# One-hot rows of four tokens by one instruction in the spreading of gates

## The chip, the cores and the metric

One core of one Trainium2 chip runs the whole program. The metric is the device time of one execution in microseconds; the kernel before took 4191.1 us in the median of three runs (4186.91 to 4193.54).

## The reference

Two layers of a decoder trunk over 512 tokens of width 1024. Each layer has a token mixer (four branches, gates, projections) and then PEER, a feed-forward network of 16384 experts, addressed by a row key and a column key out of 128 each. Only PEER bears on this change:

```
top_s, pos = lax.top_k(cand, PEER_TOPK)
eidx = jnp.take_along_axis(cidx, pos, axis=-1)      # row * 128 + column
gate = jax.nn.softmax(top_s, axis=-1)
hidden = jax.nn.gelu(jnp.einsum('td,thkd->thk', xb, u_tab[eb]))
return jnp.einsum('thk,thkd->td', gb * hidden, v_tab[eb])
```

For each token 8 heads pick 16 experts each, so there are 128 pairs (expert, gate) a token. The kernel computes all 16384 experts densely for 384 of the 512 tokens, and multiplies by a matrix of gates that is zero where an expert wasn't picked. The first 128 tokens are done by gathering their picked rows instead.

## The kernel before, in words

A layer goes through stages, each a block of its own for all engines: mixers, merge, query, routing (`route_stage`), spreading of gates (`spread_stage`), experts (`experts_stage`). The change is in `spread_stage`, which runs once in each layer.

The routing leaves three tiles of 128 x 384: `rowT`, `colT` and `gateT`. Partition p of column t holds the row key, the column key and the gate of pair p of token t. The spreading makes of each token a 128x128 matrix (row key by column key) of gates, by one matmul: the stationary operand is one-hot over the row keys of the token's 128 pairs (`hot_row`), the moving one is one-hot over the column keys, times the gate (`hot_col`), and the sum over the 128 pairs is the matrix.

The work goes in turns of STEP = 16 tokens, 24 turns a layer, and each turn in four groups of four tokens (`g` = 0 to 3). Group g has its own PSUM bank and its own four slots of `hot_row` and `hot_col`, used again in the next turn. In a turn:

- VectorE (lines 1400 to 1418) copies 16 columns of `colT`, `rowT` and `gateT` into `cols`, writes the four `hot_row` tiles of group 0 by four 128x128 compares (L1410), and all sixteen `hot_col` tiles by a compare and a multiplication in one instruction each (L1412). In every second turn it also makes a low part of expert weights by a 128x1024 subtraction, behind group 1 (L1044).
- ScalarE writes `hot_row` of group 1 another way (L1451 to L1457, distance and ReLU), evicts each bank (L1464), and makes high parts and the GELU for the experts that are computed ahead.
- GpSimd (L1389 to L1392) writes `hot_row` of groups 2 and 3: a copy of four columns of `rowT` into `rows`, a drain, and four 128x128 compares against `iota_row`, each with one column of `rows` as its scalar.
- TensorE (L1435) does the four matmuls of a group once `hot_row` and `hot_col` are there and the bank has been evicted, and half an expert chunk's multiplication behind group 1 (L86 to L88).
- SyncE stores the finished gates in DRAM and loads expert weights ahead.

All order is by semaphores written out by hand. `spread` counts groups multiplied and frees their slots; `rows_hot` counts GpSimd's groups, `rows_hot_a` ScalarE's, `cols_hot` VectorE's; `kept` counts evictions. VectorE starts group g of a turn when TensorE has multiplied group g of the turn before, and GpSimd likewise.

Of the kernel before, what the change touches and what calls it, by code (L numbers as in the profile page):

```python
# [1340 lines left out]
def spread_stage(nc, a, layer, sb, sem, bank, x, ur, load_next, iota_row, rowT, colT, gateT):  # L1341
# [5 lines left out]
    with ExitStack() as ctx:  # L1347

        ahead = HiddenAhead(nc, a, layer, ctx, sb, sem, bank, x, ur, load_next, "sp", AHEAD_ROUTE)
        hot_row = sb(ctx, "hot_row", [P, STEP, P])  # L1350
        hot_col = sb(ctx, "hot_col", [P, STEP, P])
        cols = sb(ctx, "cols", [P, 3, STEP])
        rows = sb(ctx, "rows", [P, 2, 4])
        row_of = sb(ctx, "row_of", [P, 4])
        distance = sb(ctx, "distance", [P, 4, P])
        stage = sb(ctx, "stage", [P, 2, P, TB])
        rows_hot = sem("sp_rows_hot")
        rows_hot_a = sem("sp_rows_hot_a")
        cols_hot = sem("sp_cols_hot")
        chain_a = sem("sp_chain_a")  # L1360
        spread = sem("sp_spread")
        kept = sem("sp_kept")
        stored = [sem(f"sp_stored{b}") for b in range(2)]
        chain = sem("sp_chain")
        TURNS = TB // STEP

        def unrolled(eng, body):

            def pair(m, last):
                for b in range(2):  # L1370
                    for q in range(TURNS):
                        body((2 * m + b) * TURNS + q, b, q, m, last)
            with eng.Fori(0, NTB // 2 - 1) as m:
                pair(m, False)
            pair(NTB // 2 - 1, True)

        def two_ahead(step, eng, b, q, m, last, turn):

            if q % 2 == turn and not (b == 1 and last):
                step(eng, m + b, (2 * b + q // 2 + 2) % EC)  # L1380

        with nc.Block() as block:

            @block.gpsimd
            def _(pool):
                def body(n):
                    for g in range(2, 4):
                        pool.wait_ge(spread, 4 * n + g + 1)
                        nc.gpsimd.tensor_copy(rows[:, g % 2, :], rowT[:, ds(n * STEP + 4 * g, 4)])  # L1389
                        pool.drain()  # L1390
                        for s in range(4):
                            ins = nc.gpsimd.tensor_scalar(hot_row[:, 4 * g + s, :], iota_row[:], rows[:, g % 2, s:s + 1], None, ALU.is_equal)  # L1392
                        ins.then_inc(rows_hot, 1)

                with pool.Fori(0, NTB * TURNS) as n:
                    body(n)

            @block.vector
            def _(dve):
                def body(n, b, q, m, last):  # L1400
                    dve.wait_ge(cols_hot, 4 * n + 4)
                    nc.vector.tensor_copy(cols[:, 0, :], colT[:, ds(n * STEP, STEP)])
                    nc.vector.tensor_copy(cols[:, 2, :], rowT[:, ds(n * STEP, STEP)])
                    nc.vector.tensor_copy(cols[:, 1, :], gateT[:, ds(n * STEP, STEP)]).then_inc(chain, 1)
                    dve.wait_ge(chain, n + 1)
                    for g in range(4):
                        dve.wait_ge(spread, 4 * n + g + 1)
                        if g == 0:
                            for s in range(4 * g, 4 * g + 4):
                                nc.vector.tensor_scalar(hot_row[:, s, :], iota_row[:], cols[:, 2, s:s + 1], None, ALU.is_equal)  # L1410
                        for s in range(4 * g, 4 * g + 4):
                            ins = nc.vector.tensor_scalar(hot_col[:, s, :], iota_row[:], cols[:, 0, s:s + 1], cols[:, 1, s:s + 1],  # L1412
                                                          ALU.is_equal, ALU.mult)
                        ins.then_inc(cols_hot, 1)
                        if g == 1:
                            two_ahead(ahead.low, dve, b, q, m, last, 1)

                dve.sem_inc(cols_hot, 4)
                dve.sem_inc(ahead.u_low, 4)
                for c in range(2):  # L1420
                    ahead.low(dve, 0, c)
                unrolled(dve, body)

            @block.tensor
            def _(pe):
                def body(n, b, q, m, last):
                    for g in range(4):
                        pe.wait_ge(kept, 4 * n + g + 1)
                        if g == 1:
                            pe.wait_ge(rows_hot_a, n + 1)  # L1430
                        if g >= 2:
                            pe.wait_ge(rows_hot, 2 * n + g - 1)
                        pe.wait_ge(cols_hot, 4 * n + g + 5)
                        for s in range(4):
                            mm = nc.tensor.matmul(bank[g][:, s * P:(s + 1) * P], hot_row[:, 4 * g + s, :], hot_col[:, 4 * g + s, :],  # L1435
                                                  start=True, stop=True)
                        mm.then_inc(spread, 1)
                        if g == 1:
                            part = slice(q % 2 * KT // 2, (q % 2 + 1) * KT // 2)
                            ahead.multiply(pe, m, 2 * b + q // 2, part)  # L1440

                pe.sem_inc(spread, 4)
                pe.sem_inc(ahead.h_mm, 4)
                unrolled(pe, body)

            @block.scalar
            def _(act):
                def one_hot_rows(n):

                    act.wait_ge(spread, 4 * n + 2)  # L1450
                    nc.scalar.activation(row_of[:], rowT[:, ds(n * STEP + 4, 4)], ACT.Copy).then_inc(chain_a, 1)  # L1451
                    act.wait_ge(chain_a, 2 * n + 1)
                    for s in range(4):
                        ins = nc.scalar.activation(distance[:, s, :], iota_row[:], ACT.Abs, scale=-1.0, bias=row_of[:, s:s + 1])
                    ins.then_inc(chain_a, 1)
                    act.wait_ge(chain_a, 2 * n + 2)
                    nc.scalar.activation(hot_row[:, 4:8, :], distance[:], ACT.Relu, scale=-1.0, bias=1.0).then_inc(rows_hot_a, 1)  # L1457

                def body(n, b, q, m, last):
                    two_ahead(ahead.high, act, b, q, m, last, 0)  # L1460
                    act.wait_ge(stored[b], 16 * m + 16)
                    for g in range(4):
                        act.wait_ge(spread, 4 * n + g + 5)
                        nc.scalar.activation(stage[:, b, :, q * STEP + 4 * g:q * STEP + 4 * g + 4],  # L1464
                                             bank[g][:].rearrange("p (t c) -> p c t", t=4), ACT.Copy).then_inc(kept, 1)
                        if g == 1 and not (last and b == 1 and q == TURNS - 1):
                            one_hot_rows(n + 1)
                        if g == 2 and q % 2 == 1:
                            ahead.gelu(act, m, 2 * b + q // 2)

                act.sem_inc(kept, 4)
                act.sem_inc(stored[0], 16)
                act.sem_inc(stored[1], 16)
                act.sem_inc(ahead.h_act, 4)
                for c in range(2):
                    ahead.high(act, 0, c)
                one_hot_rows(0)
                unrolled(act, body)

            @block.sync  # L1480
            def _(sp):
                def pair(m, last):
                    if not last:
                        for r in range(2):
                            ahead.load(sp, m + 1, r)
                    else:
                        ahead.load_for_next_stage(sp, AHEAD_SPREAD)
                    for b in range(2):
                        ahead.store(sp, m, b)
                        sp.wait_ge(kept, (2 * m + b) * 4 * TURNS + 4 * TURNS + 4)  # L1490
                        sp.dma_start(a["gates"][:, :, 2 * m + b], stage[:, b].rearrange("p (g c) t -> p g c t", c=EC)).then_inc(stored[b], 16)

                for r in range(2):
                    sp.sem_inc(ahead.h_out[r], 16)
                with sp.Fori(0, NTB // 2 - 1) as m:
                    pair(m, False)
                pair(NTB // 2 - 1, True)
# [864 lines left out]
```

## Time and profile before

| what | value |
|---|---|
| median of three runs | 4191.1 us |
| the profiled execution, its own time | 4191.99 us |
| its span, first to last instruction | 4190.3 us |
| mean granted TensorE clock, share of full | 0.960 |
| ScalarE busy | 1483.8 us (35%) |
| GpSimd busy | 1312.4 us (31%) |
| GpSimd `hot_row` compares L1392, 128x128, 384 of them | 254.2 us, mean 676 ns |
| VectorE `hot_row` compares L1410, 128x128, 192 of them | 44.6 us, mean 302 ns |
| TensorE `hot_col` x `hot_row` L1435, records | 1536, 191.1 us |

A row of the profile names the line, the engine, the operation, output and input tiles with their shapes, and the number of instructions. In a list in order of time the first column is the start and the second the duration in microseconds; a row with x4 stands for four instructions in a row, and the duration runs from the start of the first to the end of the last. A bracket at the end is idle time of the engine before the row, and what ended it. Instructions of one engine overlap a little: the next can start before the one ahead has ended, so the step between two starts is the time that one costs in a full queue. DVE is VectorE, POOL is GpSimd, ACT is ScalarE, PE is TensorE.

### The profile page before, as it was taken

Reading aid. Unit: us, or ns where it says so; the run is one execution under the profiler, and the core shown is the slowest. Engines: PE = TensorE matmul, PEld = TensorE weight load, DVE = VectorE, ACT = ScalarE, POOL = GpSimd, SP = SyncE. Lnnn points to the kernel's source line nnn. Section 1 sums busy time; section 2 is a strip of 40 time slices with the busy share of each in tenths; the row PEclk is TensorE's granted clock in tenths of the full one; section 3 lists DMA queues with packets and bytes.
Section 4 is the critical chain, followed back from the end, with each engine's and each line's share of the span. In section 5 each row is a group of like instructions: output and inputs, shape, how many; then the busy total and the mean of one; then the engine's idle time right before and its main releaser. Section 6 shows DMA issues by size and latency. Waiting matters only on the chain. (4 is left out here: it accounts for less than half of the span.)

```text
span 4190.3 us, 55217 instructions
## 1 busy us (share of the span) xinstructions
PE 3896.6 (93%) x19618; PEld 3407.1 (81%) x19618; DVE 2799.5 (67%) x5400; ACT 1483.8 (35%) x2136; POOL 1312.4 (31%) x1140
## 2 busy tenths in 40 slices
PE   8987899999789999999899878999997899999996
PEld 7865687899788999988778566878997889999885
DVE  3254434479997888877642644343899888888776
ACT  2232322234573333333321323222445633333332
POOL 1010000056574555532100100000666755555321
PEclk9997899999899999999999978999999999999998
DMA  3210323244369999999622103222444699999994
GB/s 141 80 57 1 111 93 113 106 149 174 124 217 360 354 354 338 345 338 333 234 102 80 58 1 118 96 103 106 160 168 147 231 358 355 358 340 344 334 331 173
DMA packets 263243, 836.41 MB, mean 200 GB/s; under 512 B 19617, under 2 KB 68769, under 8 KB 237985
## 3 DMA queue, kind: packets, MB, share of 16 engines
q1 hardware_dynamic: 189344, 565.82, 37.8%
q0 software_dynamic: 73728, 268.47, 17.4%
q8 instruction: 89, 1.46, 0.1%
q14 instruction: 82, 0.66, 0.0%
HBM read 749.81 MB, written 84.41 MB: 199 GB/s over the span
## 5 line engine op out<-in xcount | busy, mean ns | idle before, releaser
L1044 POOL TENSOR_TENSOR ahead_u_low<-merged,ahead_u_high 128x1024 fp32r<-128x1024 f32 x96 | 255.5, 2678 | 1241.4 <-ACT ahead_u_high L1039 1241.4
L87 PE MATMUL bank<-v_high,w_high 128*128 128x512 f32 x1536 | 598.1, 389 | 0.0
L86 PE MATMUL bank<-v_low,w_high 128*128 128x512 f32 x1536 | 598.1, 389 | 0.0
L88 PE MATMUL bank<-v_high,w_low 128*128 128x512 f32 x1536 | 597.4, 389 | 0.0
L1089 POOL DMA_INDIRECT far_rows<-peer_v_dram,far_index x256 | 370.4, 1447 | 503.5 <-DVE x_far L1113 458.9
L1089 POOL DMA_INDIRECT far_rows<-peer_u_rows_dram,far_index x256 | 368.0, 1437 | 346.0 <-DVE far_dots L1095 295.4
L1731 DVE TENSOR_TENSOR v_low<-v_raw,v_high 128x1024 fp32r<-128x1024 f32 x256 | 301.9, 1221 | 231.4 <-ACT v_high L1670 231.4
L1670 ACT ACTIVATE v_high<-v_raw 128x1024 fp32r<-128x1024 f32 x256 | 257.1, 1052 | 499.0 <-PE bank L88 493.4
L86 PE MATMUL bank<-xT_low,u_high 128*128 128x384 f32 x1088 | 372.1, 342 | 19.2 <-ACT hid L1658 10.0
L88 PE MATMUL bank<-xT_high,u_low 128*128 128x384 f32 x1088 | 371.2, 341 | 0.0
L87 PE MATMUL bank<-xT_high,u_high 128*128 128x384 f32 x1088 | 371.1, 341 | 0.0
L1113 DVE SCALAR_TENSOR_TENSOR x_far<-far_rows,far_dots,x_far 128x1024 f32<-128x1024 f32 x256 | 328.1, 1282 | 23.6 <-DMA far_rows<-peer_v_dram,far_index 10.0
L88 PEld LDWEIGHTS bank<-v_high,w_low 128*128 128x128 f32 x1536 | 288.4, 188 | 60.4
L86 PEld LDWEIGHTS bank<-v_low,w_high 128*128 128x128 f32 x1536 | 288.4, 188 | 59.2
L87 PEld LDWEIGHTS bank<-v_high,w_high 128*128 128x128 f32 x1536 | 288.4, 188 | 58.5
L86 PE MATMUL bank<-xT_low,ahead_u_high 128*128 128x384 f32 x960 | 329.5, 343 | 0.0
L87 PE MATMUL bank<-xT_high,ahead_u_high 128*128 128x384 f32 x960 | 324.0, 337 | 0.0
L88 PE MATMUL bank<-xT_high,ahead_u_low 128*128 128x384 f32 x960 | 323.9, 337 | 0.0
L1095 DVE CUSTOM_DVE_ANT_0 far_rows<-far_rows,x_far 128x1024 f32<-128x1024 f32 x256 | 302.5, 1220 | 18.6 <-DMA far_rows<-peer_u_rows_dram,far_index 18.1
L1664 ACT ACTIVATE w_high<-hid 128x384 fp32r<-128x384 f32 x256 | 128.9, 526 | 443.2 <-DVE hid L1722 443.2
L1392 POOL TENSOR_SCALAR hot_row<-iota_row,rows 128x128 f32<-128x128 f32 x384 | 254.2, 676 | 16.3 <-issue 16.3
L1435 PE MATMUL bank<-hot_col,hot_row 128*128 128x128 f32 x1536 | 191.1, 281 | 40.3 <-DVE hot_col L1412 22.9
(356 smaller groups left out, 8520.4 us busy)
## 6 DMA issues: line engine op xcount, KB each, us to landing
merged<-peer_u_dram SPq DMA_DIRECT2D x128, 1024.0 KB, 7.2
v_raw<-peer_v_dram SPq DMA_DIRECT2D x128, 1024.0 KB, 7.9
gates_scratch<-stage SPq DMA_DIRECT2D x12, 4096.0 KB, 14.4
G<-gates_scratch SPq DMA_DIRECT2D x64, 768.0 KB, 7.8
in_raw<-w_in_dram SPq DMA_DIRECT2D x40, 1024.0 KB, 6.2
mg_raw<-w_merge_dram SPq DMA_DIRECT2D x52, 768.0 KB, 4.2
hidden_scratch<-ahead_hid SPq DMA_DIRECT2D x60, 384.0 KB, 2.4
hid<-hidden_scratch SPq DMA_DIRECT2D x30, 768.0 KB, 7.1
```

Source lines behind the costliest of these rows:

```text
L86: nc.tensor.matmul(out, lh, rl, start=first, stop=False)
L87: nc.tensor.matmul(out, lh, rh, start=False, stop=False)
L88: return nc.tensor.matmul(out, ll, rh, start=False, stop=last)
L1044: eng.tensor_tensor(self.ul[:, c], self.ur[:, c], as_f32(self.uh[:, c]), ALU.subtract).then_inc(self.u_low, 1)
L1089: pool.indirect_dma_start(self.rows[:, m % RING, :], None, self.tables[m // PAIRS], bass.IndirectOffsetOnAxis(ap=self.index[:, slot:slot + ...
L1095: self.nc.vector.tensor_tensor_reduce(out=row, in0=row, in1=self.x[:], scale=1.0, scalar=0.0, op0=ALU.mult, op1=ALU.add, accum_out=self.do ...
L1113: self.nc.vector.scalar_tensor_tensor(out=self.x[:], in0=self.rows[:, m % RING, :], scalar=self.dots[:, m - PAIRS:m - PAIRS + 1], in1=self ...
L1392: ins = nc.gpsimd.tensor_scalar(hot_row[:, 4 * g + s, :], iota_row[:], rows[:, g % 2, s:s + 1], None, ALU.is_equal)
L1435: mm = nc.tensor.matmul(bank[g][:, s * P:(s + 1) * P], hot_row[:, 4 * g + s, :], hot_col[:, 4 * g + s, :], start=True, stop=True)
L1664: A(wh[:, b, c, :], hid[:, b, c, :], ACT.Copy).then_inc(w_high, 1)
L1670: A(vh[:, c:c + 2, cols(r)], vr[:, c:c + 2, cols(r)], ACT.Copy).then_inc(v_high, 1)
L1731: V.tensor_tensor(vl[:, c:c + 2, cols(r)], vr[:, c:c + 2, cols(r)], as_f32(vh[:, c:c + 2, cols(r)]), ALU.subtract).then_inc(v_low, 1)
```

## The change

GpSimd's copy into `rows` and its four 128x128 compares a group become two instructions of 128x512. The first subtracts the four tokens' row keys, each repeated over 128 columns, from `iota_row`, repeated four times, with both operands read from SBUF by patterns with a step of zero. The second, behind the drain, compares the result in place with 0.0. VectorE's four 128x128 compares of group 0 become one 128x512 compare of the same two patterns, and its copy of `rowT` into `cols` goes. The tile `rows` goes, and `cols` is a third smaller. Nothing changes in the waits and the counts, nor in the column compares.

```
             def _(pool):
                 def body(n):
                     for g in range(2, 4):
+                        four = hot_row[:, 4 * g:4 * g + 4, :]
                         pool.wait_ge(spread, 4 * n + g + 1)
-                        nc.gpsimd.tensor_copy(rows[:, g % 2, :], rowT[:, ds(n * STEP + 4 * g, 4)])
+                        nc.gpsimd.tensor_tensor(four, iota_row[:].unsqueeze(1).to_broadcast([P, 4, P]),
+                                                rowT[:, ds(n * STEP + 4 * g, 4)].unsqueeze(2).to_broadcast([P, 4, P]),
+                                                ALU.subtract)
                         pool.drain()
-                        for s in range(4):
-                            ins = nc.gpsimd.tensor_scalar(hot_row[:, 4 * g + s, :], iota_row[:], rows[:, g % 2, s:s + 1], None, ALU.is_equal)
-                        ins.then_inc(rows_hot, 1)
+                        nc.gpsimd.tensor_scalar(four, four, 0.0, None, ALU.is_equal).then_inc(rows_hot, 1)
...
                     nc.vector.tensor_copy(cols[:, 0, :], colT[:, ds(n * STEP, STEP)])
-                    nc.vector.tensor_copy(cols[:, 2, :], rowT[:, ds(n * STEP, STEP)])
                     nc.vector.tensor_copy(cols[:, 1, :], gateT[:, ds(n * STEP, STEP)]).then_inc(chain, 1)
...
                         if g == 0:
-                            for s in range(4 * g, 4 * g + 4):
-                                nc.vector.tensor_scalar(hot_row[:, s, :], iota_row[:], cols[:, 2, s:s + 1], None, ALU.is_equal)
+                            nc.vector.tensor_tensor(hot_row[:, 0:4, :], iota_row[:].unsqueeze(1).to_broadcast([P, 4, P]),
+                                                    rowT[:, ds(n * STEP, 4)].unsqueeze(2).to_broadcast([P, 4, P]), ALU.is_equal)
```

## Rows read from the trace of the kernel before

**Rows 1.** The page's first part: busy time of each engine.
```profile
PE 3896.6 (93%) x19618; PEld 3407.1 (81%) x19618; DVE 2799.5 (67%) x5400; ACT 1483.8 (35%) x2136; POOL 1312.4 (31%) x1140
```

**Rows 2.** Busy time by stretch: the stage in each layer.
```profile
core 0: us, PE busy (x) PEld busy (x) DVE busy (x) ACT busy (x) POOL busy (x), PEclk, DMA share, GB/s
1088.10:1249.50 161.40, 144.51 (x1056) 142.01 (x1056) 148.88 (x563) 116.36 (x258) 133.02 (x237) 0.96 0.53 182
3174.10:3332.40 158.30, 142.82 (x1056) 140.51 (x1056) 148.73 (x563) 116.18 (x258) 133.82 (x237) 0.97 0.54 186
```

**Rows 3.** VectorE in order of time, two turns: start, us, engine, line, operation.
```profile
1195.94 0.17 DVE L1402 COPY cols<-colT 128x16 f32<-128x16 f32 x1
1196.03 0.17 DVE L1403 COPY cols<-rowT 128x16 f32<-128x16 f32 x1
...
1196.31 0.91 DVE L1410 TENSOR_SCALAR hot_row<-iota_row,cols 128x128 f32<-128x128 f32 x4
1197.13 4.49 DVE L1412 TENSOR_SCALAR hot_col<-iota_row,cols 128x128 f32<-128x128 f32 x16
1201.66 0.31 DVE L1402 COPY cols<-colT 128x16 f32<-128x16 f32 x1
...
1202.26 0.98 DVE L1410 TENSOR_SCALAR hot_row<-iota_row,cols 128x128 f32<-128x128 f32 x4
1203.16 2.21 DVE L1412 TENSOR_SCALAR hot_col<-iota_row,cols 128x128 f32<-128x128 f32 x8
1205.30 1.21 DVE L1044 TENSOR_TENSOR ahead_u_low<-merged,ahead_u_high 128x1024 fp32r<-128x1024 f32 x1
...
1208.85 0.17 DVE L1402 COPY cols<-colT 128x16 f32<-128x16 f32 x1
```

**Rows 4.** GpSimd in order of time, same stage, first layer.
```profile
1154.14 0.24 POOL L1389 COPY rows<-rowT 128x4 f32 x1 [5.66 <-PE bank L1435]
...
1201.58 2.39 POOL L1392 TENSOR_SCALAR hot_row<-iota_row,rows 128x128 f32<-128x128 f32 x4 [0.17 <-issue]
1204.78 0.26 POOL L1389 COPY rows<-rowT 128x4 f32 x1 [0.81 <-PE bank L1435]
1205.21 3.50 POOL L1392 TENSOR_SCALAR hot_row<-iota_row,rows 128x128 f32<-128x128 f32 x4 [0.17 <-issue]
```

**Rows 5.** VectorE in order of time: mixers and routing.
```profile
256.25 2.31 DVE L2169 COPY tmp<-tmp 128x6 f32<-128x6 f32 x1
...
881.70 0.68 DVE L1287 TENSOR_TENSOR hits<-best 128x512 f32<-128x512 f32 x1
882.30 0.55 DVE L1290 TENSOR_TENSOR hits<-best 128x384 f32<-128x384 f32 x1
...
892.10 1.61 DVE L1308 TENSOR_TENSOR pgate<-top 128x128 f32<-128x128 f32 x1
...
894.75 0.29 DVE L1315 TENSOR_TENSOR rankf<-rankf 128x128 f32<-128x128 f32 x1
```

**Rows 6.** GpSimd in order of time, beside rows 5.
```profile
256.14 4.73 POOL L1873 TENSOR_TENSOR gl_wl<-gl_raw,gl_wh 128x1024 fp32r<-128x1024 f32 x2 [4.93 <-ACT gl_wh L1869]
...
891.16 2.40 POOL L1044 TENSOR_TENSOR ahead_u_low<-merged,ahead_u_high 128x1024 fp32r<-128x1024 f32 x1 [1.75 <-ACT ahead_u_high L1039]
```

**Rows 7.** GpSimd's groups by line and shape: count, busy us, mean ns.
```profile
L1922 POOL TENSOR_SCALAR_AFFINE_SELECT ws<-ws 128x512 f32<-128x512 f32 x2 | 1.3, 630 | 0.0
L169 POOL TENSOR_SCALAR_AFFINE_SELECT lvl_mask<-lvl_mask 128x128 f32<-128x128 f32 x4 | 1.2, 308 | 0.3
```

**Rows 8.** VectorE in order of time, while GpSimd waits.
```profile
1150.01 0.88 DVE L1410 TENSOR_SCALAR hot_row<-iota_row,cols 128x128 f32<-128x128 f32 x4
1150.80 2.14 DVE L1412 TENSOR_SCALAR hot_col<-iota_row,cols 128x128 f32<-128x128 f32 x8
1152.86 1.22 DVE L1044 TENSOR_TENSOR ahead_u_low<-merged,ahead_u_high 128x1024 fp32r<-128x1024 f32 x1
```

**Rows 9.** VectorE's groups by line and shape: the column compare.
```profile
L1412 DVE TENSOR_SCALAR hot_col<-iota_row,cols 128x128 f32<-128x128 f32 x768 | 215.6, 352 | 0.1
```

More of the change, by code:

```diff
@@ L1351, in spread_stage @@
         hot_col = sb(ctx, "hot_col", [P, STEP, P])
-        cols = sb(ctx, "cols", [P, 3, STEP])
-        rows = sb(ctx, "rows", [P, 2, 4])
+        cols = sb(ctx, "cols", [P, 2, STEP])
         row_of = sb(ctx, "row_of", [P, 4])
```

## The prediction

> **What bounds the kernel now.** The page's first part [rows 1] shows TensorE busy 93% of the span and VectorE 67%, an average over stages with different limits. The change touches one stage only, so I went on to the table of busy time by stretches for the two times it runs (once for each layer) [rows 2]: 161.4 and 158.3 us, 319.7 us of 4190.3. In it VectorE is busy 148.9 of 161.4 us and GpSimd 133.0. A layer has 24 turns of 16 tokens, so a turn takes 6.7 us on average.
>
> Next comes VectorE in order of time, for two turns late in the first layer [rows 3]. The reader is to see that it never stops: a turn that begins at 1195.94 ends at 1201.66 (5.72 us), the next one, with a 128x1024 subtraction in it, ends at 1208.85 (7.19 us). No row has an idle time. 12.91 us for two turns, 6.45 for one: VectorE sets the pace. GpSimd in the same stretch [rows 4] is nearly as full: four compares of 128x128 take 2.39 us, each group pays 0.17 us for the drain, and it waits 0.81 us for TensorE once in two turns. So anything that is added to VectorE in this stage lengthens it at once, and about 0.4 us a turn is what GpSimd could lose before it binds too.
>
> **What the change removes from VectorE.** One copy of 128x16, 0.09 us from its start to the next one's (1195.94 to 1196.03). Four one-hot compares of 128x128: 0.82 us (1196.31 to 1197.13) and 0.90 us (1202.26 to 1203.16), mean 0.86 [rows 3]. It adds one compare of 128x512 with two tensor inputs. A 128x512 operation on two SBUF inputs with broadcast patterns is in the trace: it starts at 881.70, and the next one at 882.30 [rows 5], so 0.60 us. VectorE's own work falls by 0.09 + 0.86 - 0.60 = 0.35 us a turn.
>
> **What it does on GpSimd.** Out: a copy of 128x4, and four compares of 128x128, for each of two groups a turn. In: a subtraction of 128x512 with two tensor inputs, the drain (stays at 0.17 us), and one compare of 128x512 against a constant. No row shows either at that size. The subtraction: 128x1024 takes 2.40 us in [rows 6]. Half of it, 1.2 us, is the low bound, the whole 2.4 the high one; the nearest row is twice its size, so I take 1.3. The compare: GpSimd's one-input operation of 128x512 (affine select) takes 630 ns and that of 128x128 308 ns [rows 7], 0.84 ns a column; a 128x128 compare takes 600 ns undisturbed (2.39 us for four, [rows 4]), so 0.60 + 384 x 0.00084 = 0.92 us; low bound 0.63 us (the affine select), high bound 2.4 us (four times the small one). A group takes 1.3 + 0.17 + 0.92 = 2.4 us, against 0.43 (copy and drain, 1204.78 to 1205.21, [rows 4]) + 2.39 = 2.8 before. By its own work GpSimd gains 0.4 us a group.
>
> **What the two do to each other.** This is the term that decides. At 256.14 GpSimd begins two subtractions of 128x1024, 4.73 us together [rows 6]. At 256.25 VectorE begins a copy of six columns, and it takes 2.31 us [rows 5]. At 891.16 GpSimd begins another one, which ends at 893.56; a VectorE operation of 128x128 that began at 892.10 ends at 893.71, after 1.61 us, where a like one takes 0.29 (894.75). So VectorE stands still until GpSimd's whole instruction is through, and then has 0.15 us to go: of its own 0.29 us, 0.14 were spent while it waited. The other way round, GpSimd's four compares take 3.50 us instead of 2.39 when VectorE's subtraction of 1.21 us falls into them (1205.21 in [rows 4], 1205.30 in [rows 3]).
>
> Now, why does the stage not suffer from this today, with GpSimd comparing all the time? Because the compares are short. With GpSimd idle (it waits 5.66 us until 1154.14, [rows 4]) VectorE's four row compares take 0.79 us and eight column compares 2.06 (1150.80 to 1152.86, [rows 8]), 0.257 us each; with GpSimd at work sixteen take 4.49 (1197.13 to about 1201.62, [rows 3]) instead of 4.11. That is 0.38 us on sixteen plus about 0.07 on the four; 0.45 us spread over eight GpSimd compares is 0.056 us for each. Nearly all of the 600 ns of a small compare leaves VectorE free.
>
> After the change GpSimd has four long instructions in a turn instead of eight short ones. For the subtraction I take the part that shuts VectorE out as half of 2.31 us, 1.16 us, less the 0.14 us that VectorE spends usefully: 1.02 us. Bounds: 0 (if these patterns don't shut it out) and 2.2. For the compare: what a small one costs, 0.056, plus 384 columns at 0.84 ns, 0.38 us. Bounds: 0 and its whole duration of 0.92. Two groups a turn: 2 x (1.02 + 0.38) = 2.80 us. The 0.38 us of today's disturbance on the column compares goes. Net for a turn: 2.80 - 0.38 - 0.35 = +2.07 us, a turn of 8.5 us. The first turn of a layer has its GpSimd groups ahead of VectorE's work and the last turn's fall largely behind it, so 23 turns in each of the two layers pay: 46 x 2.07 = +95 us.
>
> Is GpSimd or TensorE then the bound in place of VectorE? GpSimd: 4.8 us for two groups, 0.6 for the mean share of VectorE's 1.2 us subtraction, about 0.5 for its new compare: 5.9 of 8.5. TensorE is busy 144.5 us in 24 turns [rows 2], 6.0 us a turn, and has room. What waits behind VectorE's stalled compare is its column compares, the group's matmuls after them, and ScalarE's eviction; all of them are late by the same amount and none adds. The stage's block ends before the next stage works, and that one's load of the gates waits for the last store, so I find nothing that gives the time back.
>
> The Trainium skill, "SBUF — State Buffer", section "Who interferes with whom", speaks against this change: GpSimd shares a port pair with VectorE, and whichever starts first holds it for the whole of its instruction, against VectorE's two-input operations and its two-port modes (which it lists tensor_scalar under). The rows agree for a copy and for two-input operations; for VectorE's tensor_scalar against a long GpSimd instruction the trace of before has no row. By the rule taken literally, with each GpSimd instruction's whole duration, the small compares of today would have to stop VectorE for 0.6 us each, and what was worked out above from the rows is 0.056.
>
> The same skill, "GPSIMD Engine Reference", section 3.1, gives 4497 ns for a two-input operation of 2048 columns. An estimate from that page with this trace's 2.40 us for 1024 is 1.37 us for 512 columns; put in for 1.3 it would move the sum by under 8 us.
>
> **The time.** The profiled execution took 4191.99 us (span 4190.3) and the median is 4191.1, so they can be read as one. 4192 + 95 = 4287 us, in the median's terms 4286.
>
> **Rivals.**
> A. The port is shared only against operations with two tensor inputs and copies, and VectorE's tensor_scalar compares pass beside GpSimd (no row shows one stopped for long; the 0.056 us may be other things). Then VectorE saves 0.35 us a turn, GpSimd 0.8, and TensorE with 6.0 is close behind: 48 x 0.35 = 17 us less, 4175. Against it: the column compares do get slower when GpSimd is at work. It decides if column compares keep their mean [rows 9]. Chance 0.10.
> B. Only the subtraction shuts VectorE out, the compare against a constant doesn't, or the waits fall into gaps: 2 x 1.02 - 0.73 = 1.31 us a turn, +60, 4252. For it: a small compare leaves VectorE free for most of its duration. Chance 0.20.
> C. GpSimd's instructions hold it for their whole duration: 2 x (1.3 - 0.14 + 0.92) - 0.73 = 3.43 us a turn, +158, 4350. For it: the copy at 256.25 was stopped 0.11 us after GpSimd's start. Chance 0.15.
> D. The compare of 128x512 costs four small ones, 2.4 us, and holds as long: GpSimd 2 x 3.9 us a turn, VectorE's 5.7 plus 2 x (1.02 + 2.3) = 12.3 a turn, +5.9, +270, 4460. Chance 0.05.
> The forecast has 0.50. TensorE's clock could add to C and D: granted 0.96 and 0.97 of full on average in this stage [rows 2]; a turn with more idle time may see the lower of its two levels (1.2 GHz) more often. I give that no price of its own.
>
> The range reaches from 4235, below B, to 4355, just past C; outside are A and D and a little of B: 0.2. A measurement of this kernel can tell 0.2%, 8.4 us, from no change. Slower: forecast, B, C, D, 0.90, less a little for mishaps between A and B: 0.88. Faster: most of A, 0.09. Same: 0.03.
>
> **What would show it.** In the changed profile: the mean of VectorE's 128x128 column compare, 352 ns before [rows 9], rises to about 500 ns (2.8 us over sixteen and the rest), with single ones over 1 us; GpSimd's subtraction near 1.3 us and its compare near 0.9; the stage some 48 us longer in each layer; TensorE's waits in it for VectorE's column tiles. Wrong is the whole reasoning if the column compares stay at 350 ns. Wrong in its sizes only if they rise and GpSimd's two instructions differ from 1.3 and 0.9. Equal stage times with a slower VectorE would mean that it was not the bound.

## The result

The changed kernel took 4265.92 us in the median (4262.55 to 4268.86, 4 runs) against 4192.32 us of the kernel before (4186.91 to 4194.08, 4 runs). The ratio is 1.0179, 95% interval 1.0162 to 1.0195: slower by 74 us. The profiled execution took 4262.55 us, its span is 4260.9. A second series, beside the experiments, gave 4269.27 us and a ratio of 1.0185 (1.0170 to 1.0201).

### The profile page after: what moved, and what is told of

It is laid out like the page before. It is cut to its first block and busy times, and to the rows that moved or that the text cites. A ratio compares the mean times of both kernels' runs of the same rounds, so it can differ in the third digit from the quotient of the medians.

```text
span 4260.9 us, 54737 instructions
## 1 busy us (share of the span) xinstructions
PE 3923.5 (92%) x19618; PEld 3424.4 (80%) x19618; DVE 2877.6 (68%) x5208; ACT 1486.5 (35%) x2136; POOL 1304.4 (31%) x852
## 5 line engine op out<-in xcount | busy, mean ns | idle before, releaser
L1411 DVE TENSOR_SCALAR hot_col<-iota_row,cols 128x128 f32<-128x128 f32 x768 | 300.9, 498 | 1.5 <-PE bank L1434 1.5
L1434 PE MATMUL bank<-hot_col,hot_row 128*128 128x128 f32 x1536 | 217.3, 295 | 84.3 <-DVE hot_col L1411 73.2
```

## The profile after

The page's first part doesn't say where the loss is. GpSimd's busy time even fell, from 1312.4 [rows 1] to 1304.4 us. VectorE's rose by 78 us with 192 instructions fewer, which says that they got longer, but not which.

```profile
PE 3923.5 (92%) x19618; PEld 3424.4 (80%) x19618; DVE 2877.6 (68%) x5208; ACT 1486.5 (35%) x2136; POOL 1304.4 (31%) x852
```

The table of busy time by stretches, for the same stage in both layers (from VectorE's first copy to the end of the last eviction; columns as in [rows 2]):

```profile
1086.20:1283.50 197.30, 160.32 (x1056) 152.51 (x1056) 187.66 (x467) 117.73 (x257) 128.29 (x94) 0.92 0.44 149
3203.00:3402.60 199.60, 161.13 (x1056) 153.34 (x1056) 187.62 (x467) 117.61 (x257) 127.64 (x94) 0.91 0.43 147
```

161.4 and 158.3 us have become 197.3 and 199.6: 319.7 us have become 396.9, +77.2. The rest of the span went from 3870.6 to 3864.0 us. In the ten profiles of the experiments, worked out in the same way, that rest lies between 3864.0 and 3873.6 us, so its 6.6 us are scatter. The whole loss is in the stage.

VectorE in order of time, from the middle of the first layer (columns as in [rows 3]):

```profile
1126.72 0.69 DVE L1408 TENSOR_TENSOR hot_row<-iota_row,rowT 128x512 f32<-128x512 f32 x1 [0.21 <-DVE cols L1403]
1127.33 2.14 DVE L1411 TENSOR_SCALAR hot_col<-iota_row,cols 128x128 f32<-128x128 f32 x8
1129.39 1.22 DVE L1044 TENSOR_TENSOR ahead_u_low<-merged,ahead_u_high 128x1024 fp32r<-128x1024 f32 x1
1130.67 4.05 DVE L1411 TENSOR_SCALAR hot_col<-iota_row,cols 128x128 f32<-128x128 f32 x8
1134.86 0.57 DVE L1402 COPY cols<-colT 128x16 f32 x1
1135.35 0.16 DVE L1403 COPY cols<-gateT 128x16 f32 x1
1135.72 0.69 DVE L1408 TENSOR_TENSOR hot_row<-iota_row,rowT 128x512 f32<-128x512 f32 x1 [0.21 <-DVE cols L1403]
1136.33 6.55 DVE L1411 TENSOR_SCALAR hot_col<-iota_row,cols 128x128 f32<-128x128 f32 x16
1143.03 0.17 DVE L1402 COPY cols<-colT 128x16 f32 x1
```

GpSimd in the same stretch:

```profile
1130.83 1.08 POOL L1389 TENSOR_TENSOR hot_row<-iota_row,rowT 128x512 f32<-128x512 f32 x1 [6.41 <-PE bank L1434]
1132.08 1.53 POOL L1393 TENSOR_SCALAR hot_row<-hot_row 128x512 f32<-128x512 f32 x1 [0.17 <-issue]
1133.57 1.07 POOL L1389 TENSOR_TENSOR hot_row<-iota_row,rowT 128x512 f32<-128x512 f32 x1
1134.80 1.49 POOL L1393 TENSOR_SCALAR hot_row<-hot_row 128x512 f32<-128x512 f32 x1 [0.16 <-issue]
1136.53 1.04 POOL L1389 TENSOR_TENSOR hot_row<-iota_row,rowT 128x512 f32<-128x512 f32 x1 [0.24 <-PE bank L1434]
1137.73 1.52 POOL L1393 TENSOR_SCALAR hot_row<-hot_row 128x512 f32<-128x512 f32 x1 [0.16 <-issue]
1139.22 1.06 POOL L1389 TENSOR_TENSOR hot_row<-iota_row,rowT 128x512 f32<-128x512 f32 x1
1140.45 1.53 POOL L1393 TENSOR_SCALAR hot_row<-hot_row 128x512 f32<-128x512 f32 x1 [0.16 <-issue]
```

The reader is to see three things. While GpSimd waits (6.41 us until 1130.83) eight column compares take 2.14 us, as in [rows 8]. Once it works, eight take 4.05 us and sixteen take 6.55, with the same work in each. And the slow ones lie where GpSimd's rows lie: four long instructions between 1130.83 and 1136.3 or between 1136.53 and 1142. Even a copy of 16 columns (1134.86) takes 0.57 us instead of 0.17; a GpSimd compare had begun 0.06 us ahead of it. In the lists by line and shape, the row that answers to [rows 9], and VectorE's new compare:

```profile
L1411 DVE TENSOR_SCALAR hot_col<-iota_row,cols 128x128 f32<-128x128 f32 x768 | 300.9, 498 | 1.5 <-PE bank L1434 1.5
...
L1408 DVE TENSOR_TENSOR hot_row<-iota_row,rowT 128x512 f32<-128x512 f32 x48 | 40.9, 851 | 7.7 <-DVE cols L1403 6.8 <-PE bank L1434 0.4
```

VectorE's new compare took 0.69 us in the rows above and 851 ns on average: it is held up at times as well.

The list of one line gives the shortest, the median and the longest of them, first before and then after. The median hardly moved, from 336 to 341 ns; the longest went from 423 to 1220 ns, and the long ones are what stands behind the mean of 498:

```profile
L1412 DVE TENSOR_SCALAR hot_col<-iota_row,cols x768: 329/336/423, 1089.5 to 3327.3; 128x128 f32<-128x128 f32 x192
L1411 DVE TENSOR_SCALAR hot_col<-iota_row,cols x768: 327/341/1220, 1088.4 to 3397.4; 128x128 f32<-128x128 f32 x192
```

## The experiments

Each was timed against the kernel before on the same chip. "Stage" is the sum of the stage's two stretches in the profiled execution, measured as above; 319.7 us before.

| kernel | median us | ratio, 95% interval | stage us |
|---|---|---|---|
| VectorE's part alone | 4192.19 | 1.0001 (0.9992 to 1.0010) | 319.4 |
| GpSimd's part alone | 4279.26 | 1.0212 (1.0198 to 1.0226) | 408.2 |
| without GpSimd's compare | 4232.89 | 1.0098 (1.0083 to 1.0114) | 356.7 |
| without GpSimd's subtraction | 4203.26 | 1.0029 (1.0019 to 1.0038) | 334.3 |
| the change again | 4269.27 | 1.0185 (1.0170 to 1.0201) | 397.1 |
| half a subtraction more | 4296.42 | 1.0245 (1.0229 to 1.0261) | 428.0 |
| two groups on VectorE | 4194.62 | 1.0006 (0.9997 to 1.0015) | 324.6 |
| before, compares from PSUM | 4217.38 | 1.0060 (1.0045 to 1.0075) | 350.0 |
| the same again | 4216.82 | 1.0060 (1.0044 to 1.0077) | 349.8 |
| changed, compares from PSUM | 4210.58 | 1.0046 (1.0029 to 1.0063) | 343.2 |

**VectorE's part alone.** GpSimd's loop is that of the kernel before, VectorE's that of the changed one. Against the changed kernel:

```
-                        nc.gpsimd.tensor_tensor(four, iota_row[:].unsqueeze(1).to_broadcast([P, 4, P]),
-                                                rowT[:, ds(n * STEP + 4 * g, 4)].unsqueeze(2).to_broadcast([P, 4, P]),
-                                                ALU.subtract)
+                        nc.gpsimd.tensor_copy(rows[:, g % 2, :], rowT[:, ds(n * STEP + 4 * g, 4)])
                         pool.drain()
-                        nc.gpsimd.tensor_scalar(four, four, 0.0, None, ALU.is_equal).then_inc(rows_hot, 1)
+                        for s in range(4):
+                            ins = nc.gpsimd.tensor_scalar(hot_row[:, 4 * g + s, :], iota_row[:], rows[:, g % 2, s:s + 1], None, ALU.is_equal)
+                        ins.then_inc(rows_hot, 1)
```

> VectorE's part of the change alone; GpSimd as before with its short compares. Theory (VectorE sets the pace and GpSimd is close behind, and a two-input VectorE operation stops GpSimd): VectorE saves 0.35 us a turn, but its new 128x512 compare stops GpSimd for about 0.5 us a turn, and GpSimd had only 0.4 us spare, so between 0 and -10 us. Rival (only VectorE's own work counts): 48 x 0.35 = -17 us. Rival (the two-input compare itself is what made the change slow): +70 us.

No change. VectorE in order of time, and then GpSimd, from its late turns:

```profile
1190.78 0.23 DVE L1402 COPY cols<-colT 128x16 f32<-128x16 f32 x1
...
1191.12 0.69 DVE L1408 TENSOR_TENSOR hot_row<-iota_row,rowT 128x512 f32<-128x512 f32 x1
1191.73 3.34 DVE L1411 TENSOR_SCALAR hot_col<-iota_row,cols 128x128 f32<-128x128 f32 x12
1195.79 1.25 DVE L1411 TENSOR_SCALAR hot_col<-iota_row,cols 128x128 f32<-128x128 f32 x4 [0.71 <-PE bank L1434]
...
1203.73 0.23 DVE L1402 COPY cols<-colT 128x16 f32<-128x16 f32 x1
```

```profile
1191.18 0.68 POOL L1389 COPY rows<-rowT 128x4 f32 x1
1192.03 2.44 POOL L1392 TENSOR_SCALAR hot_row<-iota_row,rows 128x128 f32<-128x128 f32 x4 [0.17 <-issue]
1194.41 0.19 POOL L1389 COPY rows<-rowT 128x4 f32 x1
1194.78 2.42 POOL L1392 TENSOR_SCALAR hot_row<-iota_row,rows 128x128 f32<-128x128 f32 x4 [0.17 <-issue]
...
1200.73 0.83 POOL L1389 COPY rows<-rowT 128x4 f32 x1 [0.45 <-PE bank L1434]
```

VectorE's own work did get shorter: the rows of group 0 step on after 0.61 us (1191.12 to 1191.73) where four compares took 0.86 [rows 3]. But it now waits 0.71 us for TensorE, and two turns still take 12.95 us (1190.78 to 1203.73) against 12.91 before. GpSimd goes on without a stop for three groups (copy, 2.44 us, copy, 2.42 us and so on) and then waits 0.45 us for TensorE, once in two turns. VectorE's new compare (from 1191.12) also holds GpSimd up: the copy at 1191.18 takes 0.68 us, the next one 0.19. So the small reserve that [rows 4] showed was real: VectorE and GpSimd were nearly level, each now waits a little for groups that the other has a part in, and the saving on VectorE alone was worth nothing here. Which of these waits uses up how much of it is not shown. The rival of -17 us falls, and so does that of +70: VectorE's two-input compare doesn't slow the kernel.

**GpSimd's part alone.** The other half. Against the changed kernel:

```
+                    nc.vector.tensor_copy(cols[:, 2, :], rowT[:, ds(n * STEP, STEP)])
...
-                            nc.vector.tensor_tensor(hot_row[:, 0:4, :], iota_row[:].unsqueeze(1).to_broadcast([P, 4, P]),
-                                                    rowT[:, ds(n * STEP, 4)].unsqueeze(2).to_broadcast([P, 4, P]), ALU.is_equal)
+                            for s in range(4 * g, 4 * g + 4):
+                                nc.vector.tensor_scalar(hot_row[:, s, :], iota_row[:], cols[:, 2, s:s + 1], None, ALU.is_equal)
```

> GpSimd's part of the change alone; VectorE as before. Theory (GpSimd's long instructions shut VectorE out): slower by at least as much as the whole change (+74 us), +75 to +95, since the saving on VectorE is missing. Rival (GpSimd's new pair costs nothing by itself and VectorE's two-input compare does the harm): within 10 us of before.

+88 us, more than the whole change, so the rival of no more than 10 us falls. All of the loss comes with GpSimd's two instructions; VectorE's part takes 10 us of it back (the change again, on the same chip: 4269.27), 0.24 us a turn by the stage times, (408.2 - 396.9) / 48, instead of the 0.35 predicted.

**Without GpSimd's compare.**

```
-                                                ALU.subtract)
-                        pool.drain()
-                        nc.gpsimd.tensor_scalar(four, four, 0.0, None, ALU.is_equal).then_inc(rows_hot, 1)
+                                                ALU.subtract).then_inc(rows_hot, 1)
```

> The change without GpSimd's compare of 128x512 (left out, so the rows hold distances and the gates are not the reference's) and without the drain; the subtraction stays. From the changed trace a subtraction makes VectorE's compares late by 0.73 us and a compare by about 0.46. Theory (each GpSimd instruction has its own price to VectorE): 2 x 0.73 - 0.73 = +0.73 us a turn, +35 us. Rival (only the length of GpSimd's chain counts, VectorE's waits are hidden): a group takes 1.1 us instead of 2.8, so no slower than before.

+42 us, the stage +37.0. VectorE and then GpSimd in one turn in which two subtractions fall into the sixteen column compares:

```profile
1116.73 5.70 DVE L1409 TENSOR_SCALAR hot_col<-iota_row,cols 128x128 f32<-128x128 f32 x16
1122.57 0.17 DVE L1400 COPY cols<-colT 128x16 f32 x1
```

```profile
1116.71 2.04 POOL L1389 TENSOR_TENSOR hot_row<-iota_row,rowT 128x512 f32<-128x512 f32 x2 [5.01 <-PE bank L1432]
```

Undisturbed, sixteen would end 4.2 us after they began (16 x 0.257 us and the end of the last one, 0.08); here it is 5.70. So the two, 2.04 us together, cost VectorE 1.5 us, 0.75 each. Over the stage: 37.0 us + 48 turns x 0.73 us that the change saves otherwise = 72, over 96 subtractions 0.75 us. The two ways agree. GpSimd's chain was much shorter than before and idle for most of the time, and the kernel was slower all the same; the rival falls.

**Without GpSimd's subtraction.**

```
-                        nc.gpsimd.tensor_tensor(four, iota_row[:].unsqueeze(1).to_broadcast([P, 4, P]),
-                                                rowT[:, ds(n * STEP + 4 * g, 4)].unsqueeze(2).to_broadcast([P, 4, P]),
-                                                ALU.subtract)
+                        nc.gpsimd.tensor_copy(rows[:, g % 2, :], rowT[:, ds(n * STEP + 4 * g, 4)])
                         pool.drain()
-                        nc.gpsimd.tensor_scalar(four, four, 0.0, None, ALU.is_equal).then_inc(rows_hot, 1)
+                        nc.gpsimd.tensor_scalar(four, iota_row[:].unsqueeze(1).to_broadcast([P, 4, P]), 0.0, None, ALU.is_equal).then_inc(rows_hot, 1)
```

> The change with GpSimd's subtraction left out: GpSimd copies four row keys as before, and one 128x512 instruction compares the column numbers with 0.0, so the rows are wrong and the gates with them; its length and its place are those of the change. Theory (the compare of 128x512 takes 1.5 us but keeps VectorE out for only about 0.46 of them): 2 x 0.46 - 0.73 = +0.2 us a turn, +9 us. Rival (a GpSimd instruction holds the port for its whole duration): 2 x (1.5 - 0.14) - 0.73 = +2 us a turn, +95 us.

+12 us, the stage +14.6. VectorE, and GpSimd in the same turn:

```profile
1128.98 5.28 DVE L1410 TENSOR_SCALAR hot_col<-iota_row,cols 128x128 f32<-128x128 f32 x16
1134.40 0.17 DVE L1401 COPY cols<-colT 128x16 f32 x1
```

```profile
1129.27 1.49 POOL L1392 TENSOR_SCALAR hot_row<-iota_row 128x512 f32<-128x512 f32 x1 [0.16 <-issue]
...
1131.10 1.49 POOL L1392 TENSOR_SCALAR hot_row<-iota_row 128x512 f32<-128x512 f32 x1 [0.16 <-issue]
```

Two compares of 1.49 us fall into the sixteen, which take 5.28 instead of 4.2: 1.1 us for the two and the small copy between them, 0.5 us each. Over the stage (14.6 + 35) / 96 = 0.52 us. A GpSimd compare of 1.49 us costs VectorE a third of its duration, a subtraction of 1.04 us nearly three quarters. The rival, the whole duration for both, falls.

**The change again.**

> The whole change, unaltered, on the chip and beside the runs of the other three: +74 us by every theory.

+78 us, and a stage of 397.1 us: the same as the first profile of it.

**Half a subtraction more.**

```
+                        nc.gpsimd.tensor_tensor(spare[:], iota_row[:].unsqueeze(1).to_broadcast([P, 2, P]),
+                                                rowT[:, ds(n * STEP + 4 * g, 2)].unsqueeze(2).to_broadcast([P, 2, P]),
+                                                ALU.subtract)
...
```

> The whole change, and ahead of each GpSimd subtraction another one of 128x256 of the same operands into a spare tile. Theory (what is subtracted on GpSimd is lost to VectorE, in proportion to the columns): half of 0.73 us more for each of two groups a turn, +35 us over the changed kernel, +110 over before. Rival (what counts is that GpSimd's group is late for TensorE, and there is room there): no more than the changed kernel, +75.

+105 us, and the stage is 31.1 us over the changed kernel's: 0.32 us for each of 96 instructions of 256 columns, against 0.75 for 512. In proportion, or somewhat less. The rival, no slower than the changed kernel, falls.

**Two groups on VectorE.** Against VectorE's part alone (its row compare goes by `g` too):

```
-                    for g in range(2, 4):
+                    for g in range(3, 4):
...
-                        if g == 0:
+                        if g in (0, 2):
...
-                        if g >= 2:
-                            pe.wait_ge(rows_hot, 2 * n + g - 1)
+                        if g == 3:
+                            pe.wait_ge(rows_hot, n + 1)
```

> Group 2's rows made by VectorE as well, with the change's 128x512 compare; GpSimd makes group 3 alone, with the short compares of before. Theory: VectorE alone binds again, its work is 6.45 - 0.35 + 0.60 us less half of the 0.45 us that GpSimd's short compares cost it, 6.5 us a turn, so within 5 us of before; if the two-input compares also free TensorE from waiting for GpSimd, up to 10 us faster. Rival (two-input operations are what slows the stage): slower by 30 us or more.

+3 us, with 0 in the interval. VectorE pays for one more 128x512 compare a turn with what it no longer loses to GpSimd. It is no better than the kernel before; neither is any other kernel here. The rival of 30 us or more falls.

**The port, by way of PSUM: the control.** VectorE's column compares read the column numbers from a PSUM bank instead of SBUF. Groups 2 and 3 share a bank to free one.

```
+                nc.vector.tensor_copy(iota_ps, iota_row[:]).then_inc(iota_in, 1)      # iota_ps = bank[3][:, 0:P]
...
-                            ins = nc.vector.tensor_scalar(hot_col[:, s, :], iota_row[:], cols[:, 0, s:s + 1], cols[:, 1, s:s + 1],
+                            ins = nc.vector.tensor_scalar(hot_col[:, s, :], iota_ps, cols[:, 0, s:s + 1], cols[:, 1, s:s + 1],
...
-                        pe.wait_ge(kept, 4 * n + g + 1)
+                        pe.wait_ge(kept, 4 * n + (1, 2, 4, 7)[g])
```

> The kernel before, with VectorE's column compares reading the column numbers from PSUM (a bank made free by letting groups 2 and 3 share one), so that they take one input port and no SBUF read. The control for the next one. Both theories: the compares get some 0.05 to 0.1 us longer each, and groups 2 and 3 wait for each other's eviction: +20 to +90 us.

> The control again, on the same chip as the run that it stands beside: the time of the first control.

+26 and +24 us, each against the kernel before on its own chip; the two medians are 0.6 us apart.

**The port, by way of PSUM: the changed kernel.** The same edit on the changed kernel.

> The changed kernel with the same edit as the control: the column compares read PSUM. Theory (VectorE and GpSimd share an SBUF port, and an operation with no SBUF tensor input in a one-port mode does not need it): the column compares keep one duration while GpSimd works, and the change costs next to nothing: within 20 us of the control. Rival (GpSimd's long instructions slow VectorE in some other way, or by making GpSimd's groups late): again +70 us over the control.

The change no longer costs anything: 4210.58 us against the control's 4216.82 on the same chip, 6 us less, and a stage of 343.2 against 349.8 us. The theory had it within 20 us of the control, the rival 70 us above it. VectorE in one turn, and GpSimd in the same:

```profile
1118.22 5.19 DVE L1413 TENSOR_SCALAR hot_col<-bank,cols 128x128 f32<-128x128 f32 x16
1123.56 0.36 DVE L1404 COPY cols<-colT 128x16 f32 x1
```

```profile
1118.54 1.04 POOL L1391 TENSOR_TENSOR hot_row<-iota_row,rowT 128x512 f32<-128x512 f32 x1 [0.37 <-PE bank L1438]
1119.74 1.49 POOL L1395 TENSOR_SCALAR hot_row<-hot_row 128x512 f32<-128x512 f32 x1 [0.16 <-issue]
1121.20 1.04 POOL L1391 TENSOR_TENSOR hot_row<-iota_row,rowT 128x512 f32<-128x512 f32 x1
1122.40 1.49 POOL L1395 TENSOR_SCALAR hot_row<-hot_row 128x512 f32<-128x512 f32 x1 [0.16 <-issue]
```

Four long GpSimd instructions run from 1118.54 to 1123.9, and the sixteen compares take 5.19 us. That is 0.32 us each, dearer than the 0.257 from SBUF, but less than the 6.55 us that sixteen took beside the same four in the changed kernel. The lists of the one line, for the changed kernel and for the control, have no long ones left (shortest, median, longest):

```profile
L1413 DVE TENSOR_SCALAR hot_col<-bank,cols x768: 393/402/415, 1089.0 to 3345.6; 128x128 f32<-128x128 f32 x192
```

```profile
L1414 DVE TENSOR_SCALAR hot_col<-bank,cols x768: 390/399/408, 1087.6 to 3349.9; 128x128 f32<-128x128 f32 x192
```

The longest is 415 ns where it was 1220. GpSimd's instructions, their lengths and their place in the order are those of the changed kernel; only where VectorE reads its input is different. So what the two engines contend for goes with VectorE's reading from SBUF, and it is not GpSimd's lateness. Whether it is the read itself, or the quicker working from SBUF (0.257 against 0.32 us), this pair can't tell: the edit changes both. The Trainium skill, "SBUF — State Buffer", section "Who interferes with whom", says that a VectorE operation with at most one SBUF input, outside the two-port modes, does not contend with GpSimd. This pair of runs agrees, with 415 ns at the longest. The same section of the Trainium skill says of VectorE's two-port modes that the engine that comes second is blocked for the other's whole instruction. For the subtraction that is nearly so (0.75 of 1.04 us lost), for GpSimd's compare these runs show 0.5 of 1.49 us, and the measurement decides.

## Why the prediction was right, step by step

- **VectorE sets the pace, with GpSimd 0.4 us a turn behind.** Right. VectorE's part alone shortened its work and not the kernel; GpSimd's part alone lengthened VectorE's and the kernel.
- **VectorE saves 0.35 us a turn.** Its row compare steps on after 0.61 us, 0.60 was taken. Of the 0.35 us only 0.24 came through in the changed kernel, and nothing in VectorE's part alone.
- **The lengths of GpSimd's instructions** were both off. The subtraction: 1.3 us predicted, 1.04 to 1.08 measured. The compare: 0.92 predicted, 1.49 to 1.53 measured, because the price of a column was taken from the affine select [rows 7] and doesn't carry over to it. A group by its own work takes 1.06 + 0.16 + 1.5 = 2.7 us, nearly the 2.8 of before, and not 2.4. Neither length is a term of the forecast's sum, so these two misses moved nothing in it. The prediction's other estimate of the subtraction, 1.37 us, comes out as 1.35 when it is worked again, and is no nearer.
- **What shuts VectorE out.** The mechanism was right, rival A (the column compares pass) is refuted by the 1220 ns and by the PSUM pair. The sizes: 1.02 us for a subtraction, measured 0.75, since the subtraction is over in 1.04 to 1.08 us and not 1.16, and of the 0.99 us that a stopped compare takes to the next start (in the last section) 0.257 are its own work, not 0.14; 0.38 for a compare, measured 0.5. The two misses partly cancel, which is luck: 1.40 us a group predicted, 1.25 measured.
- **The sum.** +2.07 us a turn was predicted for 46 turns, +95 us; the stage grew by 77.2 us, 1.61 for each of 48 turns, and the kernel by 74. The term that was mis-sized is the subtraction's: 0.27 us too much, twice a turn, is 25 us; the compare's, 0.12 too little, takes 11 of them back. 95 - 25 + 11 = 81. One reading in the sum was off too: the 0.38 us of disturbance before sets 4.49 us, which runs to the end of the last compare, beside 4.11, which doesn't; with its last 0.08 us the disturbance is 0.30, and the sum 4 us more. What is left between that and 77.2 us no run assigns.
- **Nothing gives it back.** Right: the rest of the span is the same within its scatter. TensorE was busy 160 of 197 us, at a granted clock of 0.92 and 0.91 instead of 0.96 and 0.97. Whether the clock has a share in the loss was not tried by itself; the PSUM pair, at 0.98 and 0.97 in most of the stage, has it back along with the time. It can hardly be a large one: in the first layer's stage of the changed kernel VectorE waited for TensorE 1.1 us in all.
- **What would show it.** The mean of the column compare was to rise to about 500 ns with single ones over 1 us; it is 498, with 1220.
- **Rivals B and C.** B had the compare free for VectorE; it costs 0.5 us. C had both at their whole length; the compare keeps VectorE out for a third of it. The measured time lies between the forecast and B because of the subtraction, not because the compare was free.

## What to carry to other kernels

Merging small instructions on GpSimd can cost more than it saves if VectorE works beside it: look at the longest instance, not the median, of each VectorE operation, and set it beside GpSimd's rows in order of time. A small GpSimd compare cost VectorE 0.056 us, 0.45 us for a turn's eight; four long instructions cost 2.5 us. And where two engines were level within 0.4 us a turn, shortening the work of one of them was worth nothing.

## What was not expected

GpSimd's 128x512 compare against a constant took 1.49 us, 2.4 times its affine select of the same shape (0.63 us), and more than its two-input subtraction of the same shape (1.04 us), yet it cost VectorE less, 0.5 against 0.75 us. The subtraction of 512 columns took less than half of that of 1024 (2.40 us, fp32r output). The rows of the changed kernel show when GpSimd's compare lets VectorE through. These are VectorE's column compares one by one (the one that begins at about 1133.24 is left out), beside GpSimd's three instructions from 1130.83, 1132.08 and 1133.57:

```profile
1130.93 1.07 DVE L1411 TENSOR_SCALAR hot_col<-iota_row,cols 128x128 f32<-128x128 f32 x1
1131.92 0.34 DVE L1411 TENSOR_SCALAR hot_col<-iota_row,cols 128x128 f32<-128x128 f32 x1
1132.17 0.63 DVE L1411 TENSOR_SCALAR hot_col<-iota_row,cols 128x128 f32<-128x128 f32 x1
1132.72 0.34 DVE L1411 TENSOR_SCALAR hot_col<-iota_row,cols 128x128 f32<-128x128 f32 x1
1132.98 0.70 DVE L1411 TENSOR_SCALAR hot_col<-iota_row,cols 128x128 f32<-128x128 f32 x1
...
1133.67 1.05 DVE L1411 TENSOR_SCALAR hot_col<-iota_row,cols 128x128 f32<-128x128 f32 x1
```

The one that meets the subtraction (1130.93) is stopped until the subtraction is over (1131.91): 0.99 us to the next start instead of 0.257. Beside GpSimd's compare (1132.08 to 1133.61) the first is held up, 0.55 us to the next start; the next one passes in 0.26; and the two after it take 0.69 us together instead of 0.51, the first of them not ending before GpSimd's compare does. So the compare keeps VectorE out at its beginning (0.29 us lost) and at its end (0.18), and hardly between. That makes 0.47 us, which agrees with the 0.5 of the experiment. What GpSimd does in these two stretches no run here shows.
